# Part of an MLP's first multiplication in a seven-product form, inside a fused two-block kernel on Trainium2

## The reference

```python
h2 = rmsnorm(x, norm2_g)                      # (256, 2048)
x = x + jnp.square(jax.nn.relu(h2 @ w_mlp_in)) @ w_mlp_out
```

## Time and profile before

| | us |
|---|---|
| median of 3 runs | 2855.16 (2854.54 to 2856.0) |
| the profiled execution | 2855.43 |
| its span on the core | 2853.7 |
| TensorE matmul, busy | 2836.7 (99%) |
| VectorE, busy | 1841.6 (65%) |
| ScalarE, busy | 1367.8 (48%) |

### The profile page before, as it was taken

How to read it: one execution, slowest core, us unless ns; L and a number is a source line. 1 busy time by engine, 2 the same in 40 slices (tenths; PEclk the granted TensorE clock), 3 DMA queues, 4 the chain that set the end, 5 groups by cost and what they waited for, 6 DMA issues and landing times.

```text
span 2853.7 us, 33235 instructions
## 1 busy us (share of the span) xinstructions
PE 2836.7 (99%) x13330; PEld 2343.4 (82%) x13330; DVE 1841.6 (65%) x1965; ACT 1367.8 (48%) x1524; POOL 2.1 (0%) x7
## 2 busy tenths in 40 slices
PE   9999999999999999999999999999999999999998
PEld 7888878888888888888888888887888888888887
DVE  7698855656765555555567669876766655556555
ACT  6644446644455444444455444444455444444444
POOL 0000000000000000000000000000000000000000
PEclk9999999999999999999999999999999999999999
DMA  9576656666777666666667666666677666666664
GB/s 319 160 221 196 207 171 203 194 192 197 250 237 221 192 202 220 202 213 192 210 215 230 213 209 201 201 200 212 208 221 233 210 213 193 211 195 221 203 205 168
DMA packets 361498, 596.51 MB, mean 209 GB/s; under 512 B 21888, under 2 KB 95232, under 8 KB 360704
## 3 DMA queue, kind: packets, MB, share of 16 engines
q1 hardware_dynamic: 360912, 594.06, 66.6%
q10 hardware_dynamic: 432, 0.32, 0.0%
HBM read 556.81 MB, written 2.10 MB: 196 GB/s over the span
## 4 chain that ended last, share of the span: by engine, by line
PE 95%; DVE 3%; DMA 1%; issue 1%; ACT 1%; SPq 0%; DVEq 0%; ACTq 0%
PE ACC L707 94%; DVE WL L1347 1%; DMA RAW<-in_w_in_dram 0%; ACT WH L915 0%; PE TB L767 0%; DMA RAW<-in_w_c_out_dram 0%; DVE HT L1792 0%; DVE ZCb L1767 0%; DVE MG L1772 0%; DVE WGC L1983 0%; DVE CA L1935 0%; PE TB L800 0%; PE TB L803 0%; PE TB L832 0%; PE TB L809 0%
## 5 line engine op out<-in xcount | busy, mean ns | idle before, releaser
L1347 DVE TENSOR_TENSOR WL<-RAW,WH 128x1024 fp32r<-128x1024 f32 (+1 forms) x1023 | 1229.6, 1217 | 798.0 <-ACT WH L915 794.0
L915 ACT ACTIVATE WH<-RAW 128x1024 fp32r<-128x1024 f32 (+1 forms) x1023 | 1065.8, 1054 | 1185.7 <-PE ACC L707 811.2
L707 PE MATMUL ACC<-WH,XTH 128*128 128x512 f32 (+1 forms) x1692 | 658.6, 389 | 6.6 <-DVE WL L1347 3.1
L707 PE MATMUL ACC<-WL,XTH 128*128 128x512 f32 (+1 forms) x1692 | 655.1, 387 | 0.0
L707 PE MATMUL ACC<-WH,XTL 128*128 128x512 f32 (+1 forms) x1692 | 655.1, 387 | 0.0
L707 PE MATMUL ACC<-WH,XBH 128*128 128x512 f32 x1024 | 398.4, 389 | 0.0
L707 PE MATMUL ACC<-WL,XBH 128*128 128x512 f32 x1024 | 398.4, 389 | 0.0
L707 PE MATMUL ACC<-WH,XBL 128*128 128x512 f32 x1024 | 398.4, 389 | 0.0
L707 PEld LDWEIGHTS ACC<-WH,XTH 128*128 128x128 f32 x1692 | 317.8, 188 | 75.8 <-DVE WL L1347 4.8
L707 PEld LDWEIGHTS ACC<-WH,XTL 128*128 128x128 f32 x1692 | 317.8, 188 | 65.1
L707 PEld LDWEIGHTS ACC<-WL,XTH 128*128 128x128 f32 x1692 | 317.9, 188 | 63.8
(11 more groups left out here) (276 smaller groups left out, 1599.0 us busy)
## 6 DMA issues: line engine op xcount, KB each, us to landing
RAW<-in_w_in_dram SPq DMA_DIRECT2D x255, 512.0 KB, 4.3
RAW<-in_w_mlp_in_dram SPq DMA_DIRECT2D x128, 512.0 KB, 4.0
RAW<-in_w_mlp_out_dram SPq DMA_DIRECT2D x128, 512.0 KB, 4.8
RAW<-in_w_up_dram SPq DMA_DIRECT2D x128, 512.0 KB, 4.2
RAW<-in_w_down_dram SPq DMA_DIRECT2D x128, 512.0 KB, 4.8
RAW<-in_w_gate_dram SPq DMA_DIRECT2D x96, 512.0 KB, 4.4
YT<-HT SPq DMA_DIRECT2D x208, 128.0 KB, 2.7
RAW<-in_w_branch_dram SPq DMA_DIRECT2D x48, 512.0 KB, 4.2
```

Source lines behind the costliest of these rows:

```text
L707: ins = e.matmul(ACC[:, 2 * (b % 2) + half, 0:n], p[:, k, xs], q[:, t, 0:n], start=(k == 0 and m == 0), stop=(k == nk - 1 and m == 2))
L915: e.activation(WH[u % NSPL][:, :, 0:n], RAW[u % NRAW][:, :, 0:n], ACT.Copy).then_inc(hi, 1)
L1347: e.tensor_tensor(l, r, h, ALU.subtract).then_inc(lo, 1)
```

## The change

Up blocks (j, 0) and (j, 1) with j of 1 to 7 become pairs, in both MLPs: 14 pairs. The 16 units of a pair alternate between the two blocks: unit (i, m) has tiles 2i and 2i+1 of block m. The two units of an i are a quad: two token halves, two tiles, two column blocks, thus eight block products of three matmuls. For i of 1, 4 and 6 (42 quads in all) the eight become seven. TensorE multiplies sums of input quarters (`SXR`, made once for each MLP) with sums of weight tiles (`TS`, made for each quad); products that are used several times gather in the four `ACC` banks, the others and all ordinary quads in `TB0` to `TB3`. When the pair ends, VectorE adds the gathered products together and adds `TB` times the row scale. Since the gathered products would come out without the row scale, the sums of inputs have it (or a ratio of the halves' scales) in them, for which a product with a diagonal matrix spreads the scale over the partitions.

In short, by engine, of a seven-product quad of units (i, 0), (i, 1): TensorE 6 matmuls in the first unit, 15 in the second; VectorE four sums, 128x512 each, then the low part of half a unit and the low parts of the sums, 128x1024 twice; ScalarE two high parts of sums, 128x1024 each, before the high part of the second unit's remaining half.

```diff
+    SEVEN_I = (1, 4, 6)
...
+        paired = name[0] in ("h1", "h2") and name[1] > 0
...
+        f = first("h" + tag, 0, 0)
+        at(("xs", tag), f + 4)
+        at(("rsb", tag), f + 5)
+        at(("xs", tag), f + 6, 5)
+        at(("xs_hi", tag), f + 11)
+        at(("xs", tag), f + 12)
...
+                end = last("h" + tag, j, 1)
+                at(("mid", tag), end - 2 + b)
+                at(("end", tag), end + b)
+                at(("ev", "h" + tag), end + 1 + b)
+                turn_at(("h" + tag, j, b), end + 3 + b, 9)
...
             if u >= NRAW:
                 e.wait_ge(lo, u - NRAW + 1)
+                if u - NRAW in SEVEN:
+                    e.wait_ge(t_sum, 4 * SEVEN[u - NRAW][0] + 4)
...
+            e.wait_ge(lo, u + 1)
...
+            if m == 0:
+                if new:
+                    e.wait_ge(acc[b0 % 2], b0 // 2)
+                three(acc_bank(b0, 0), sums(S_A), w[0], new, end)
+                three(TB[0][:, :], x(2 * i + 1, 0), w[1], False, False).then_inc(mm, 1)
+                return
+            three(TB[1][:, :], sums(S_4), w[1], False, False)
+            if new:
+                e.wait_ge(acc[(b0 + 1) % 2], (b0 + 1) // 2)
+            e.wait_ge(t_lo, 2 * q + 1)
+            three(acc_bank(b0 + 1, 0), sums(S_1), weight_sums(T1), new, end)
+            three(acc_bank(b0 + 1, 1), sums(S_3), weight_sums(T3), new, end)
+            e.wait_ge(t_lo, 2 * q + 2)
+            three(acc_bank(b0, 1), sums(S_2), weight_sums(T2), new, end)
+            three(TB[2][:, :], x(2 * i + 1, 1), weight_sums(T4), False, False).then_inc(mm, 1)
...
+        def sums_high(u):
+            q = SEVEN[u][0]
+            tr = TR[NAMES[units[u][0]][0][1]]
+            if q:
+                e.wait_ge(mm, SEVEN_END[q - 1] + 1)
+            for k in range(2):
+                e.wait_ge(t_sum, 4 * q + 2 * k + 2)
+                e.activation(TS[0][:, 2 * k:2 * k + 2, :], tr[:, 2 * k:2 * k + 2, :], ACT.Copy).then_inc(t_hi, 1)
...
             if u + AHEAD < NU:
                 cut(u + AHEAD)
+                if SEVEN.get(u + AHEAD, (0, 1))[1] == 0:
+                    sums_high(u + AHEAD)
...
+        def weight_sums(u):
...
+            e.wait_ge(raw[(u + 1) % NRAW], 16 * ((u + 1) // NRAW + 1))
+            e.tensor_tensor(tr[:, T1, :], b12, b11, ALU.subtract).then_inc(t_sum, 1)
+            e.tensor_tensor(tr[:, T3, :], b22, b12, ALU.subtract).then_inc(t_sum, 1)
+            e.wait_ge(t_sum, 4 * q + 1)
+            e.tensor_tensor(tr[:, T2, :], b22, tr[:, T1, :], ALU.subtract).then_inc(t_sum, 1)
+            e.wait_ge(t_sum, 4 * q + 3)
+            e.tensor_tensor(tr[:, T4, :], b21, tr[:, T2, :], ALU.subtract).then_inc(t_sum, 1)
+
+        def weight_sums_low(u):
...
+            for k in range(2):
+                f = slice(2 * k, 2 * k + 2)
+                e.wait_ge(t_hi, 2 * q + k + 1)
+                e.tensor_tensor(TS[1][:, f, :], tr[:, f, :], TS[0][:, f, :], ALU.subtract).then_inc(t_lo, 1)
...
             if u + AHEAD < NU:
                 cut(u + AHEAD)
+                if u + AHEAD in SEVEN:
+                    (weight_sums_low if SEVEN[u + AHEAD][1] else weight_sums)(u + AHEAD)
```

More of the change, by code:

```diff
@@ L117, in build @@
     mlp_blocks("2", a["w_up_2"][0], a["w_down_2"][0])
-    units, U0, UE = [], [], []
+    NAMES = list(B)
+    SEVEN_I = (1, 4, 6)
+    units, U0, UE = [], [0] * len(plan), [0] * len(plan)
+    PAIR, SEVEN = {}, {}
     for b, (w, nk, c0, n) in enumerate(plan):
-        U0.append(len(units))
-        units += [(b, i) for i in range(nk // 2)]
-        UE.append(len(units) - 1)
+        name = NAMES[b]
+        paired = name[0] in ("h1", "h2") and name[1] > 0
+        if paired and name[2] == 1:
+            continue
+        for i in range(nk // 2):
+            for m in range(2 if paired else 1):
+                u = len(units)
+                if i == 0:
+                    U0[b + m] = u
+                UE[b + m] = u
+                if paired:
+                    PAIR[u] = (7 * (name[0] == "h2") + name[1] - 1, b, m)
+                    if i in SEVEN_I:
+                        SEVEN[u] = (3 * PAIR[u][0] + SEVEN_I.index(i), m)
+                units.append((b + m, i))
     NU = len(units)
+    SEVEN_END = [u for u, (q, m) in SEVEN.items() if m == 1]
     def first(*name):
@@ L176, in build @@
     pool_hi = sem("pool_hi")
+    xs, xs_hi, xs_lo, diag, rsb = sem("x_sums"), sem("x_sums_hi"), sem("x_sums_lo"), sem("root_diagonal"), sem("root_rows")
+    t_sum, t_hi, t_lo = sem("weight_sums"), sem("weight_sums_hi"), sem("weight_sums_lo")
+    p1_out, mid, n_out, relu = sem("product1_out"), sem("product_sums"), sem("pair_out"), sem("pair_relu")
     x5_done, y_out, y_out_a = sem("final_gain"), sem("final_out"), sem("final_out_scalar")
@@ L182, in build @@
     X = sb("X", [P, 2, D])
-    XTH, XTL = sb("XTH", [P, 16, L], F32R), sb("XTL", [P, 16, L], F32R)
+    XTH = sb("XTH", [P, 16, L], F32R)
+    over = ExitStack()
+    XTF = sb("XTF", [P, 4096], to=over)
+    over.close()
+    XTL = sb("XTL", [P, 16, L], F32R)
     RAW = [sb(f"RAW{i}", [P, 2, 512]) for i in range(NRAW)]
@@ L709, in products, with three, pair_unit, x @@
             return ins
+        def three(dst, x, w, start, stop):
+            for m, (p, q) in enumerate(((x[0], w[0]), (x[0], w[1]), (x[1], w[0]))):
+                ins = e.matmul(dst, p, q, start=(start and m == 0), stop=(stop and m == 2))
+            return ins
+        def pair_unit(u):
+            (b, i), (n, b0, m) = units[u], PAIR[u]
+            tag = NAMES[b][0][1]
+            w = [(WH[u % NSPL][:, t, :], WL[u % NSPL][:, t, :]) for t in range(2)]
+            def x(k, half):
+                return [y[:, k, half * P:half * P + P] for y in XB[tag]]
+            if i == 0 and m == 0:
+                e.wait_ge(n_out, 4 * n)
+                e.wait_ge(xs_lo, n // 7 + 1)
+            e.wait_ge(lo, u + 1)
+            if u not in SEVEN:
+                for half in range(2):
+                    for t in range(2):
+                        ins = three(TB[2 * half + m][:, :], x(2 * i + t, half), w[t], i == 0 and t == 0, i == 7 and t == 1)
+                ins.then_inc(mm, 1)
+                return
+            q = SEVEN[u][0]
+            new, end = q % 3 == 0, q % 3 == 2
+            def sums(f):
+                return [y[:, f, q % 3, :] for y in SXR]
+            def weight_sums(f):
+                return [y[:, f, :] for y in TS]
+            if m == 0:
[3 more added lines that the diff above has]
+                three(TB[0][:, :], x(2 * i + 1, 0), w[1], False, False).then_inc(mm, 1)
+                return
+            three(TB[1][:, :], sums(S_4), w[1], False, False)
[7 more added lines that the diff above has]
+            three(TB[2][:, :], x(2 * i + 1, 1), weight_sums(T4), False, False).then_inc(mm, 1)
+        def root_rows(tag):
+            e.wait_ge(diag, 3 * int(tag))
+            e.matmul(TB[0][:, 0:3 * P], ONES, DG, start=True, stop=True).then_inc(rsb, 1)
+            yield
         def stream(u, front):
@@ L889, in _ @@
                  "pm": pool_means, "wg": pool_groups}
+        for tag in ("1", "2"):
+            tasks["rsb", tag] = lambda tag=tag: root_rows(tag)
         for n in range(4):
@@ L1185, in hidden_out, with product1_out, sums_split @@
         def hidden_out(tag, r):
-            for j in range(8):
-                for b in range(2):
[L1188 to L1197, removed]
+            for b in range(2):
+                hb, bl = HB[tag][b], B["h" + tag, 0, b]
+                if b == 0:
+                    e.wait_ge(rooted, rooted_at(r))
+                multiplied(e, "h" + tag, 0, b)
+                for half in range(2):
+                    ins = e.activation(hb[:, half, :], ACC[:, 2 * (bl % 2) + half, :], ACT.Relu, scale=RS[r][:, half:half + 1])
+                ins.then_inc(acc[bl % 2], 1)
+                evicted(e, "h" + tag, 0, b)
+                e.activation(hb[:, :, :], hb[:, :, :], ACT.Square).then_inc(hid, 1)
+                yield
+            for j in range(1, 8):
+                for b in range(2):
+                    hb, n = HB[tag][b], 7 * (tag == "2") + j - 1
+                    e.wait_ge(n_out, 4 * n + 2 * b + 2)
+                    e.activation(hb[:, :, :], hb[:, :, :], ACT.Relu).then_inc(relu, 1)
+                    e.wait_ge(relu, 2 * n + b + 1)
                     e.activation(hb[:, :, :], hb[:, :, :], ACT.Square).then_inc(hid, 1)
                     yield
+        def product1_out(tag):
+            for j in range(1, 8):
+                n = 7 * (tag == "2") + j - 1
+                e.wait_ge(turned, TN["h" + tag, j - 1, 0] + 1)
+                e.wait_ge(mm, SEVEN_END[3 * n + 2] + 1)
+                e.activation(HB[tag][0][:, 0, :], acc_bank(B["h" + tag, j, 0], 0), ACT.Copy).then_inc(p1_out, 1)
+                yield
+                yield
+        def sums_split(tag):
+            multiplied(e, "wo" + tag, 3)
+            e.wait_ge(xs, 10 * int(tag))
```

(29 more changed lines are left out.)

84 lines of the change are left out of this document (75 added, 9 removed).

## The result

The changed kernel takes 2862.39 us (median of 9 runs, 2861.41 to 2864.16) against 2855.20 us before (9 runs in the same comparison): ratio 1.0025, 95% interval 1.0015 to 1.0036. It is 7 us slower with 126 matmuls less. The forecast was 2864.

A forecast was written before the change was run, and what follows sets the result against it. TensorE, busy 99% of the span, was taken as the bound. Losses of 15.4, 7.3, 12.3 and 2.7 (37.7 us) against 28.6 gained gave net +9.1 us, so 2864 us; range 2845 to 2874.

The forecast's parts named there:

- The gain: All seven-product quads: each saves three matmuls; 126 matmuls of 0.2267 us, 28.6 us gained.
- Unit 3 of an ordinary pair: First quad: TensorE waits 0.83 us for unit 3's low part, 0.45 for the first sums; 1.28 us lost.
- Quads 4 and 6 to spare in ordinary pairs: Quads 4 and 6 of ordinary pairs: nothing lost, with 0.88 and 0.49 us to spare.
- The pair's end: Unit 22, behind VectorE's residual addition and transposes: 0.52 us lost per pair, 7.3 us over 14 pairs.
- The first pairs: First pair of each MLP: 3.8 us lost at unit 3 and sums, 2.35 later; 6.15 a pair, 12.3 total.
- the walk: Operation-by-operation timing of the engines' queues through a pair; an ordinary pair loses 1.80 of its 2.04 us.
- The later losses: First pair of each MLP, quads 4 and 6: late weights of unit 8 and a VectorE split, 2.35 us lost.
- Input sums: At j=0: 1.0 us lost at unit 11 and 0.35 for spreading the scale; 1.35, twice, 2.7 total.
- 97% busy or less: Sign in the profile after: VectorE busy near 70%, yet TensorE down to 97% or less.
- Rival (d): The clock falls in TensorE's waits: twice for a few units gives 2874 us; chance 0.02.
- Rival (a): Cushion holds at each pair's unit 3, chain 0.83 us shorter: 2849 us, 2842 with pair's end covered; chance 0.22.
- The strict reading: VectorE's next operation starts only when the pipe is empty: chain 0.3 us longer per pair, total 4 us higher.

The follow-up runs named there:

- run 2845: Changed kernel with ScalarE making unit 3's high part ahead of the high parts of the weight sums: 2845.03 us, ratio 0.9963.
- three moves: Changed kernel with unit 3's high part first, a pair's second transposes one unit later, and j=0's second-block transposes one unit later: 2841.25 us.
- the last two runs: Changed kernel with quads 2, 4, 6, high part first, both transposes later: 2829.76 us; then also input sums' unit-8 step at unit 7: 2829.07 us.

## Why the prediction was right

Point by point, by its steps:

- *The gain*, 126 x 0.2267 = 28.6 us: shown to about 1 us. With nearly all waits gone the period shrinks by 2.10 and, lined up by residual additions, the two MLPs take 27.5 us less, and that after 2 x 0.65 for spreading the scales. The spans differ by 27.0, the medians by 25.8.
- *Unit 3 of an ordinary pair*, 0.83 + 0.45 = 1.28 lost: measured 0.79 + 0.5; taking away the cause gave 1.34 a pair. All starts of the chain were within 0.05 us, and the sums took 0.60 and 0.72 as priced.
- *Quads 4 and 6 to spare in ordinary pairs*: right, no wait there.
- *The pair's end*, 0.52: 0.37 in the trace, 0.41 as the run with later transposes shows. That is most of the difference between the 1.80 forecast for a pair and the 1.69 measured (12 pairs, 1.3 us in all).
- *The first pairs*: unit 3 3.34 forecast, 3.13 and the 0.11 of the restart measured; 0.45, 0.5. By its own prices the walk has T4 at 6.41 (3.35 + 1.14 + 0.60 + 0.60 + 0.72) and not at 6.47, which its end at 7.16 asks for; the trace has 6.40. The later losses were forecast as 2.35, at quads 4 and 6, for late weights and a split. Measured were 1.0 in the first MLP and 1.6 in the second, and 0.6 of each at unit 4, where the walk had nothing: the split of the first block of j=0 stands ahead of that unit's low. The term was on average 1 us a pair too large: the weights of unit 8, behind the moves, were taken up 17.8 us after the start of `hidden_out` in the first MLP, where the sum has 19.0 (14.8 + 1.7, and 2.5 that unit 3 costs here beyond an ordinary pair).
- *Input sums*: 1.0 forecast at unit 11, 0.85 measured; 0.35 for the scales, 0.65 measured. That price came from products of 256 columns in a row and was too small.
- The sum was +9.1. Measured were +6.5 between the profiled spans and +7.2 between the medians. By stretches of the traces: ordinary pairs gave back 4.2 where the sum has 2.9; first pairs with j=0 cost 10.1 where it has 12.0; outside the MLPs 0.6 was lost where it has nothing, which no run explains. 9.1 - 1.3 - 1.9 + 0.6 is 6.5. Part of the closeness is luck, since the terms that were off partly cancel.
- I wrote that TensorE would be down to 97% busy or less. It showed 99%; the busy time is that of overlapping matmuls, and the chain was the place to look.
- *Rival (d)*, the clock: it got 0.02, and that was too little. In the profiled execution of the changed kernel the clock stood at 1.00 in both waits of 3.1 us, in other executions it probably fell; but a fall cost far less than the 5 us of the rival, see below. *Rival (a)* named the right place and a right remedy (the high of unit 3 ahead of those of the sums); it gave 2849 for that, and the run 2845.
- The strict reading of the Trainium skill's page "VectorE: DVE Perf Modes", section "The DRAIN you can't avoid", would have made the chain 0.3 us longer. The trace has the next independent operation 0.60 us after the start of one of 0.69 (1042.83 to 1043.43), and the low of unit 3 where the 0.60 puts it.

## What to carry to other kernels

When work is taken off the engine that bounds the kernel and put on one that is 65% busy, walk the queues through the tightest place, operation by operation with start-to-start times, before asking how busy they are: here the whole gain of 28.6 us and 7 more were lost that way, and moving one copy behind another gave 17 us back with the load unchanged. An operation that waits for a chain (the high part of a sum) shouldn't stand ahead of one that is ready and that the bounding engine needs first. And when an operation is moved, follow it to its new place: what stands behind it there is late next.

## What the hardware showed that I had not expected

In the run with the high part first, the wait in the first pair was 3.1 us as in the changed kernel, but behind it matmuls started 0.43 us apart and not 0.23. TensorE there:

```profile
870.67 0.39 PE L768 MATMUL TB<-WH,XBL 128*128 128x512 f32 x1
874.03 0.80 PE L768 MATMUL TB<-WH,XTH 128*128 128x512 f32 x1 [2.97 <-DVE WL L1496]
874.62 0.63 PE L768 MATMUL TB<-WL,XTH 128*128 128x512 f32 x1
875.04 0.63 PE L768 MATMUL TB<-WH,XTL 128*128 128x512 f32 x1
```

The windows from then on (after the busy times of five engines: granted clock), and then those of the changed kernel at its wait and behind it:

```profile
874.00:877.20 3.20, 3.17 (x8) 2.44 (x9) 3.20 (x3) 2.27 (x3) 0.00 (x0) 0.50 0.78 178
877.20:880.00 2.80, 2.80 (x14) 2.29 (x13) 2.80 (x4) 0.00 (x0) 0.00 (x0) 0.99 0.92 247
```

```profile
870.00:874.00 4.00, 1.02 (x5) 0.49 (x3) 4.00 (x5) 3.73 (x5) 0.00 (x0) 1.00 0.43 133
874.00:877.20 3.20, 2.94 (x13) 2.18 (x12) 3.20 (x4) 2.00 (x3) 0.00 (x0) 1.00 0.89 194
```

The granted clock was 0.50, the 1.2 GHz level, over the first of these windows and then full again. The eight matmul steps from 874.03 on took 1.5 us more than at the full clock. In the profiled execution of the changed kernel, with 3.13 us of wait too, the clock stayed at 1.00.

The other traces don't give a rule either. With the high part first it fell behind that wait in both MLPs; in the runs without sums and with later transposes it fell in the first MLP and stayed at 1.00 in the second, behind the same wait; with quads 2, 4, 6 it fell in the second MLP alone, behind a wait of 2.8 us; with three moves it fell in both, behind a wait of 2.4 us that followed one of 1.15 by some 5 us. Without such waits in the MLPs, in the last two runs, it stood up to the last microseconds, in which it is down in every trace. And with the high part first it also fell at 1938.8 us, outside the MLPs, among waits of about 2 us each that the kernel before has too, where it stood. What decides between the cases is left open by these runs.

A fall costs less than it seems to. In the run without sums the first pair with its j=0 cost 4.69 us where the clock fell and 4.32 where it didn't: 0.37 us more and not 1.5, since in the second MLP TensorE waited soon afterwards anyway (0.43 us at the first products with sums, 0.49 at unit 4), and where the matmuls were slow those waits were gone. The timed executions of the changed kernel fit this: in seven of nine the mean granted clock was 0.997 or 0.998, which was so in only two of the 22 executions of the kernel before that stand beside the experiments. So the clock probably fell in most of them, and the profiled execution (0.999) is not typical. Yet the time hardly shows it: 2861.4 to 2864.2 us for the seven, 2861.9 and 2862.0 for the other two. With three moves no wait followed the slow stretch, and a fall cost up to 1.6 us there.
